# Memory keys of the first layer beside its attention, its modulation weights in a place of their own, and two heads in turn

## The reference, cut to what matters

```python
# first stack, layer l
mod = cond @ w_mod[l] + b_mod[l]                  # 6 x 1024: shift, scale and gate, twice
h = rms_norm(x, norm_mix[l]) * (1 + sc_a) + sh_a
mq, mk, mv, dq, dk, dv = split(h @ w_in[l])       # 8 plain heads of 64, 4 differential heads (2 x 64)
x = x + g_a * (concat(moba_attention(mq, mk, mv), diff_attention(dq, dk, dv)) @ w_out[l])
x = x + g_f * ((silu(h2 @ w_gate[l]) * (h2 @ w_up[l])) @ w_down[l])
# second stack, layer l
x = x + head_group_mixer(rmsnorm(x), w_in, ...)   # 8 stick-breaking heads of 64, 4 retention heads of 128
k, v = split(rmsnorm(mem, mem_norm[l]) @ wkv[l])  # "memory": 256 x 1024, an input of its own
x = x + cross_attention(rmsnorm(x), k, v)
x = x + peer_ffn(rmsnorm(x), ...)
# stick-breaking head: z = q k' / 8, causal
log_not_b = log_sigmoid(-z); a = exp(log_sigmoid(z) + reversed cumulative sum of log_not_b)
```

## Time and profile before

| | |
|---|---|
| median of 3 runs | 2847.84 us (2845.98 to 2852.53) |
| the profiled execution | 2845.72 us, span 2843.9 us |
| mean granted TensorE clock | 0.993 of full speed |
| TensorE busy | 2767.0 us, 97% of the span |
| VectorE busy | 2099.9 us, 74% |
| ScalarE busy | 1414.8 us, 50% |
| GpSimd busy | 195.7 us, 7% |
| read from HBM | 527.48 MB, 188 GB/s over the span |

### The profile page before, as it was taken

One profiled execution on the slowest core, in us unless ns is written; L12 is line 12 of the kernel. 1 busy time (PEld: TensorE's weight loads), 2 busy tenths in 40 slices (PEclk: granted clock), 3 DMA queues, 4 the chain that ended last, 5 costly groups with the idle time before them and its releaser, 6 DMA issues.

```text
span 2843.9 us, 40048 instructions
## 1 busy us (share of the span) xinstructions
PE 2767.0 (97%) x16458; PEld 2357.3 (83%) x16458; DVE 2099.9 (74%) x3106; ACT 1414.8 (50%) x1646; POOL 195.7 (7%) x172
## 2 busy tenths in 40 slices
PE   8989999999999999999999999999999999999998
PEld 7768888788888788888888888887888888888887
DVE  7877867665553679999879955536699999799655
ACT  4454445554456555554443344484555544443443
POOL 0200002010013001210000000030011200000000
PEclk9999999999999999999999999999999999999999
DMA  8857854555553355554445555633445544455554
GB/s 331 310 182 269 320 185 173 196 178 191 192 199 134 119 179 185 187 189 164 164 166 191 177 193 192 228 125 134 171 168 190 192 165 170 157 193 176 188 195 143
DMA packets 75637, 537.41 MB, mean 189 GB/s; under 512 B 8512, under 2 KB 8896, under 8 KB 12096
## 3 DMA queue, kind: packets, MB, share of 16 engines
q1 hardware_dynamic: 75456, 534.86, 53.9%
HBM read 527.48 MB, written 7.34 MB: 188 GB/s over the span
## 4 chain that ended last, share of the span: by engine, by line
PE 65%; issue 22%; DVE 7%; ACT 4%; DMA 2%; POOL 0%; SPq 0%; DVEq 0%; POOLq 0%; ACTq 0%
PE banks L442 18%; PE banks L450 9%; PE banks L516 7%; PE banks L519 7%; PE banks L527 7%; DVE wlo L1480 3%; PE banks L490 2%; ACT whi L999 2%; PE banks L492 2%; PE banks L501 2%; PE banks L464 2%; PE banks L466 2%; PE banks L474 1%; DMA raw<-in_wkv 1%; PE banks L944 1%
## 5 line engine op out<-in xcount | busy, mean ns | idle before, releaser
L999 ACT ACTIVATE whi<-raw 128x2048 fp32r<-128x2048 f32 x438 | 838.9, 1916 | 972.5 <-issue 813.8
L1480 DVE TENSOR_TENSOR wlo<-raw,whi 128x2048 fp32r<-128x2048 f32 x438 | 1006.8, 2299 | 312.5 <-ACT whi L999 297.3
L442 PE MATMUL banks<-ht,whi 128*128 128x512 f32 x2880 | 704.8, 394 | 8.5 <-DVE big L1554 2.8
L442 PEld LDWEIGHTS banks<-ht,whi 128*128 128x128 f32 x2880 | 527.6, 189 | 113.2 <-issue 6.6
L516 PE MATMUL banks<-whi,ht 128*128 128x512 f32 x1152 | 458.1, 398 | 13.5 <-DVE ht L1544 9.0
L519 PE MATMUL banks<-whi,ht 128*128 128x512 f32 x1152 | 452.7, 393 | 0.0
L450 PEld LDWEIGHTS banks<-ht,wlo 128*128 128x128 f32 x2880 | 369.1, 191 | 14.6
L450 PE MATMUL banks<-ht,wlo 128*128 128x256 f32 x2880 | 373.4, 282 | 0.0
L527 PE MATMUL banks<-wlo,ht 128*128 128x512 f32 x1152 | 290.6, 390 | 0.0
L516 PEld LDWEIGHTS banks<-whi,ht 128*128 128x128 f32 x1152 | 217.7, 189 | 58.9 <-issue 14.6
L519 PEld LDWEIGHTS banks<-whi,ht 128*128 128x128 f32 x1152 | 217.7, 189 | 43.2
(11 more groups left out here) (274 smaller groups left out, 3425.0 us busy)
## 6 DMA issues: line engine op xcount, KB each, us to landing
raw<-in_pu SPq DMA_DIRECT2D x128, 1024.0 KB, 4.9
raw<-in_pv SPq DMA_DIRECT2D x128, 1024.0 KB, 4.9
raw<-in_win SPq DMA_DIRECT2D x52, 1024.0 KB, 5.0
big<-in_wmod SPq DMA_DIRECT2D x24, 1024.0 KB, 6.6
raw<-in_wmod SPq DMA_DIRECT2D x24, 1024.0 KB, 5.0
raw<-in_wgate SPq DMA_DIRECT2D x22, 1024.0 KB, 4.9
raw<-in_wup SPq DMA_DIRECT2D x22, 1024.0 KB, 5.2
raw<-in_wdown SPq DMA_DIRECT2D x22, 1024.0 KB, 4.9
```

What stands on the lines that cost most here:

```text
L442: m = e.matmul(bank[b + n], h[:, q, c[n]], M.both[:, q * 512:(q + 1) * 512], start=q == 0, stop=False, skip_group_check=True)
L999: e.activation(whi(j), slot[u][0], ACT.Copy).then_inc(*hi.mark(j))
L1480: e.tensor_tensor(wlo(j), slot[u][0], whi(j).bitcast(F32), ALU.subtract).then_inc(*lo.mark(j))
```

## The change

It does three things. The four key units of layer 0 move from the opening into its attention, which now is laid out as that of layer 1 (eight units, two steps each); the memory's transposes move to nb 2 and their low part to nb 3, the lead units are fetched first, and one write of layer 0's keys and values replaces two. The 16 mid units leave the ring and share one slot, `LEAD[3]`, with the next fetched when VectorE has read the last; their places in the list are spread over units 0 to 19. And two heads are taken in turn, matmul by matmul: the plain heads of the first mixer, the logits and the retention scores of the second; there `sticks`, `stick_values`, `keep` and ScalarE's functions follow in pairs, with a ring of four in place of three. On VectorE, `columns(1, 0)` moves ahead of `down(i - 1)` at one place.

```diff
--- before.py
+++ after.py
-    m0, k0 = munits(0, 0), wunits("wkv", 0, 8)
-    units += [m0[0], m0[1], k0[0], m0[2], m0[3], k0[1], m0[4], m0[5], k0[2], m0[6], m0[7], k0[3]]
-    units += first_mixer(0, [0, 1, 3, 4, 6, 7, 9, 10, 11, 12, 12, 13, 13, 14, 14, 15], munits(0, 1) + munits(0, 2))
+    units += munits(0, 0)
+    units += first_mixer(0, [0, 1, 3, 4, 6, 7, 9, 10, 11, 12, 13, 14, 15, 16, 18, 19], munits(0, 1) + munits(0, 2))
...
-    main = [u for u in range(len(units)) if u not in {*lead, *side}]
+    mid = [u for u, x in enumerate(units) if x[0] == "m" and x[2:4] in ((0, 1), (0, 2))]
+    main = [u for u in range(len(units)) if u not in {*lead, *mid, *side}]
     slot = {u: (RAW[:, i % NRAW * UN:(i % NRAW + 1) * UN], i % NRAW, i // NRAW) for i, u in enumerate(main)}
     slot.update({u: (SIDE[i % 2], NRAW + i % 2, i // 2) for i, u in enumerate(side)})
     slot.update({u: (LEAD[i], NRAW + 2 + i, 0) for i, u in enumerate(lead)})
+    slot.update({u: (LEAD[3], NRAW + 10, i) for i, u in enumerate(mid)})
...
+    order_of.update({u: (mid, i, 1) for i, u in enumerate(mid)})
...
         def first_mixer(l):
             name = ("mix1", l)
             if l == 0:
-                warm(name, 7)
-                turn_all(("m", 0), MEM, DG[1])
-                for i in range(3):
-                    if i == 2:
-                        turn_all(name, XA, DG[0])
-                    a_unit(("K", 0, i), MT, lambda q: normed(on, ("m", 0), q), b=i - 1 if i == 2 else None)
-                for _ in column_sums(0, 0, 0):
+                turn_all(name, XA, DG[0])
+                on.wait_ge(*mac.at((0, 0, 5)))
+                warm(name, 7, 0)
+                for _ in column_sums(0, 0, 1):
                     pass
-                a_unit(("K", 0, 3), MT, lambda q: normed(on, ("m", 0), q), b=2)
             else:
                 gate_row(1, 0, (0, 1))
                 warm(name, 6)
...
-                if l and nb == 2:
+                if nb == 2:
                     for t in range(2):
                         on.wait_ge(*d_mem[t].at(l))
+                    on.wait_ge(*normal.at(("m", 0, "diag")))
                     for q in range(4):
                         turn(("m", l), q, MEM, DG[1], q)
...
             def step(i):
                 if i < 8:
-                    scores(0, (i,))
+                    if i % 2 == 0:
+                        scores(0, (i, i + 1))
                 elif i < 12:
                     scores(2, (2 * (i - 8), 2 * (i - 8) + 1))
...
                         if q % 4 == 3:
-                            step(f * n)
-                    b_unit([("V", l, f // 2, t) for t in range(2)], MT, f % 2, ready, b=(2, 3),
-                           between=None if l else lambda: step(f * n + 1))
+                            step(f * 2)
+                    b_unit([("V", l, f // 2, t) for t in range(2)], MT, f % 2, ready, b=(2, 3))
                 else:
-                    a_unit(("K", l, f - 4), MT, lambda q: normed(on, ("m", l), q), lambda: step(f * n),
+                    a_unit(("K", l, f - 4), MT, lambda q: normed(on, ("m", l), q), lambda: step(f * 2),
                            (2, 3, 0, 1)[f - 4])
-                if (f + 1) * n < 12 or l:
-                    step((f + 1) * n - 1)
-
-            n = 2 if l else 3
-            for f in range(8 if l else 4):
+                step(f * 2 + 1)
+
+            for f in range(8):
                 fill(f)
-            for i in range(16 if l else 11, 16):
-                step(i)
             project(("o1", l), ("mix1", l), OO)
 
         def out_part(name, o, q, b=None):
...
-            def logits(h):
-                b = clear(("sb", l, h), 2 + h % 2)
-                on.wait_ge(*took_v.at(("f", l, 2 * (h // 4) + 1)))
-                p0, c = 64 * (h % 2), h // 2
+            def logits(c):
+                for h in (2 * c, 2 * c + 1):
+                    clear(("sb", l, h), 2 + h % 2)
+                on.wait_ge(*took_v.at(("f", l, 2 * (c // 2) + 1)))
                 for i in range(3):
-                    q = AG[p0:p0 + 64, SBQ + c * 256 + (i > 0) * 128:][:, 0:128]
-                    k = AG[p0:p0 + 64, SBK + c * 256 + (i > 1) * 128:][:, 0:128]
-                    m = e.matmul(bank[b][:, i * 128:(i + 1) * 128], k, q, start=i == 0, stop=True, skip_group_check=True)
-                m.then_inc(*scored.mark(("sb", l, h)))
+                    for h in (2 * c, 2 * c + 1):
+                        p0 = 64 * (h % 2)
+                        q = AG[p0:p0 + 64, SBQ + c * 256 + (i > 0) * 128:][:, 0:128]
+                        k = AG[p0:p0 + 64, SBK + c * 256 + (i > 1) * 128:][:, 0:128]
+                        m = e.matmul(bank[2 + h % 2][:, i * 128:(i + 1) * 128], k, q, start=i == 0, stop=True,
+                                     skip_group_check=True)
+                        if i == 2:
+                            m.then_inc(*scored.mark(("sb", l, h)))
...
-                q = [AG[p0:p0 + 64, RQ + c * 512 + i * 256:][:, 0:256] for i in range(2)]
-                k = [AG[p0:p0 + 64, RK + c * 512 + i * 256:][:, 0:256] for i in range(2)]
+                q, k = ([[AG[64 * j:64 * j + 64, x + c * 512 + i * 256:][:, 0:256] for i in range(2)] for j in range(2)]
+                        for x in (RQ, RK))
                 for i in range(2):
-                    e.matmul(bank[b][:, 0:256], k[i][:, 0:128], q[i], start=i == 0, stop=i == 1, skip_group_check=True)
+                    for j in range(2):
+                        e.matmul(of[j][:, 0:256], k[j][i][:, 0:128], q[j][i], start=i == 0, stop=i == 1,
+                                 skip_group_check=True)
                 for i in range(2):
-                    m = e.matmul(bank[b][:, 256:384], k[i][:, 128:256], q[i][:, 128:256], start=i == 0, stop=i == 1,
-                                 skip_group_check=True)
-                m.then_inc(*scored.mark(("ret", l, h)))
+                    for j in range(2):
+                        m = e.matmul(of[j][:, 256:384], k[j][i][:, 128:256], q[j][i][:, 128:256], start=i == 0,
+                                     stop=i == 1, skip_group_check=True)
...
-                if 3 <= i < 11:
+                for h in {5: (0, 1), 7: (2, 3), 9: (4, 5), 10: (6, 7)}.get(i, ()):
+                    stick_values(h)
+                if i in (3, 5, 7, 9):
                     sticks(i - 3)
-                if 2 <= i < 10:
-                    logits(i - 2)
+                    sticks(i - 2)
+                if i in (2, 4, 6, 8):
+                    logits(i // 2 - 1)
                 if i == 11:
                     retention_scores(0)
-                    retention_scores(1)
                 if i == 12:
                     retention_values(0)
                     retention_values(1)
-                    retention_scores(2)
-                    retention_scores(3)
...
-                if i % n == 0 and i // n < (8 if l else 4):
+                if i % 2 == 0:
                     take()
-                if l == 0 and i == 13:
...
                         e.activation(ag(to + t * 512, 512), psum(key)[:, :], func, scale=RMS[:, t:t + 1]).then_inc(
                             *took_a.mark(key))
-                if 3 <= i < 11:
+                if i in (3, 5, 7, 9):
                     sticks(i - 3)
-                if 2 <= i < 10:
+                    sticks(i - 2)
+                if i in (2, 4, 6, 8):
                     logits(i - 2)
+                    logits(i - 1)
...
                 columns(l, 0)
-            turn_moved(name, l, 0, lambda: None, None if l else lambda: through(place_of[4] + 2))
+            turn_moved(name, l, 0, lambda: None, None if l else lambda: upto(0))
+
+            if l == 0:
+                lambda_sums()
 
...
-                        lambdas()
-                if l and nb == 3:
+                if l == 0 and nb == 2:
+                    lambdas()
+                if l == 0 and nb == 1:
+                    diag(("m", 0), 1, lambda: None)
+                if nb == 3:
                     for q in range(4):
                         rest(("m", l, q), COLS[:, l * 64 + 48:l * 64 + 56], MT)
                 if 1 <= nb <= 4:
...
                     rotary(i - 6)
-                if 3 <= i < 11:
-                    h = i - 3
+                for h in (i - 3, i - 2) if i in (3, 5, 7, 9) else ():
                     on.wait_ge(*took_a.at(("sb", l, h)))
-                    keep(ag(RING + (h % 3) * 768, 384), ("exp", l, h))
-                if 2 <= i < 10:
-                    h = i - 2
+                    keep(ag(RING + (h % 4) * 768, 384), ("exp", l, h))
+                for h in (i - 2, i - 1) if i in (2, 4, 6, 8) else ():
                     on.wait_ge(*took_v.at(("sb", l, h)))
-                    keep(ag(RING + (h % 3) * 768 + 384, 384), ("soft", l, h))
+                    keep(ag(RING + (h % 4) * 768 + 384, 384), ("soft", l, h))
+                if i in (6, 8):
+                    rotary(i - 6)
             head_inverse(("o2", l, 0), 8, 168)
```

(30 more changed lines are left out.)

144 lines of the change are left out of this document (52 added, 92 removed).

## The result

The changed kernel took 2882.2 us (median of 4 runs, 2874.3 to 2886.2) beside 2847.9 for the kernel before: ratio 1.0115, 95% interval 1.009 to 1.0139, so about 33 us slower. I had forecast 2842.4 with a range that ended at 2850. The profiled execution has a span of 2884.4 us and a mean granted clock of 0.985, where before had 2843.9 and 0.993.

A forecast was written before the change was run, and what follows sets the result against it. TensorE, busy for 97% of the span, was taken to bound the kernel. Opening with layer 0 -1.2, layer 1's pairs -3.0 and second mixers -1.2 gave -5.4 from 2847.8: 2842.4 us, range 2832 to 2850.

The forecast's parts named there:

- Second mixer, new waits: Second mixer: new TensorE waits of 6.0 us less one of 1.35 return 4.7 of 5.3 us saved, -0.6 a layer.
- For later pairs: Second mixer, sticks of later pairs: TensorE waits 0.5, 0.2 and 0.2 us for ScalarE's chain of the second head.
- 2.4 us: Second mixer: TensorE's wait at `stick_values(6)`, since GpSimd's cut-outs of pair 3 stand behind two rotaries of 4.2 us each.
- Gain eaten: Rival, chance 0.18: 1 us lost at each of three to five new waits, perhaps by the clock; -1 us, 2847.
- Work saved: Second mixer: paired logits save 3.4 us and paired retention scores 1.9 us of TensorE, together 5.3 us a layer.
- The opening: Opening and layer 0: projection begins at 38.8, 16.5 us earlier; output projection at 194.6 against 195.75, so -1.2 us.
- Layer 1's pairs: Layer 1's first mixer: four pairs of plain heads taken in turn save 2.7 to 3.3 us, say -3.0.
- costs VectorE nothing: Layer 0's feed-forward: `columns(1, 0)` ahead of a unit costs VectorE nothing, since the low part behind waits for that unit.
- no overlap: Rival, chance 0.02: pairs do not overlap in the second mixer, 5.3 us a layer not saved; 2853.
- the waits were not hidden: Rival, chance 0.27: new waits in layer 0's projection and the second mixer are mostly hidden; -12 us, 2836.
- The mid slot: Rival, chance 0.10: the mid units' one slot becomes the bound if landing takes over 6.2 us; +8, 2850.
- The drain: Rival, chance 0.01: each ScalarE table load brings a drain, 1.4 us idle, lengthening waits for the sticks; about 2875.

The follow-up runs named there:

- e5: The changed kernel with GpSimd's selects ahead of its rotary products and ScalarE's pair work ordered by step; 2840.3 us, ratio 0.9975 to the kernel before.
- e12: The kernel before with GpSimd products and VectorE operations added behind its last transfer, alone and at once; a product took 1.31 us alone, 3.25 beside low parts.
- e3: The changed kernel with GpSimd's selects of a pair's exponentials ahead of the rotary products; 2860.3 us, ratio 1.0052 to the kernel before.
- e4: The changed kernel with idle matmuls in the three long waits of each second mixer; 2863.4 us, ratio 1.0046 to the kernel before.
- e11: e5 with idle matmuls at two places of each first mixer; 2838.8 us, ratio 0.9959 to the kernel before.
- e2: The changed kernel with its second mixers put back as before; 2846.5 us, ratio 0.9987 to the kernel before.
- e6: The changed kernel with ScalarE's order by step alone, selects still behind the rotary products; 2853.6 us, ratio 1.0017 to the kernel before.
- e1: The kernel before with the second mixers' part of the change alone; 2881.7 us, ratio 1.0102.
- e7: The kernel before with the scores of two heads in turn in layer 1's first mixer alone; 2849.1 us, ratio 0.9998.
- e9: The kernel before with the fixed second mixers alone (pairs, ring of four, selects ahead, ScalarE by step); 2845.1 us, ratio 0.9972.

## Why the prediction was wrong

- **The step that failed** is "Second mixer, new waits": "So 6.0 - 1.35 = 4.7 us come back of 5.3: -0.6 a layer". The waits were 14.9 and not 6.0, and behind them stood some 6.5 us of lower clock, so 14.9 - 1.35 + 6.5 - 5.3 = 14.8 us a mixer were lost. Taken piece by piece:
- The 2.7 us ahead of `sticks(1)` were 2.59. That ScalarE's two chains follow one another, and with no drain behind a load, held (1.28 us, and the next begins at once).
- "For later pairs ... 0.5, 0.2 and 0.2": these three did not come. I had followed the cut-outs only. The same ScalarE queue holds the copy of the values for `stick_values(0)`, behind both chains and a high part: 4.46 us, which I had nowhere. e5 took 3.0 of them away by shortening the chain.
- "2.4 us" at `stick_values(6)` was 7.8. The place and the releaser were right; the price, "two rotaries of 4.2", was read from rows in which VectorE was idle. The hint stood in the earlier trace rows: the first product took 0.98 us, with a low part over it for 0.4, and its like 0.72. In the new order the rotaries run in a row, under whole low parts, and take turns with them (e12): 14.1 us for two in place of 8.4 makes 8.1 of the 2.4. (The sum "8.35 + 8.5 + 0.4" is 17.25 and not 17.4; nothing hangs on it.) e3 gave most of it back.
- **The clock.** "Gain eaten" priced a wait at 1 us lost behind it. It was 2.2 on average for the three long ones (e4: 6.5 a mixer).
- **Work saved:** the 5.3 us a layer held: twelve logits records took the time of six, and each two heads of retention scores 933.51 - 931.99 = 1.5 us in place of 2.47. It is why the fixed mixer is shorter than before's, by 3.9 us in e5's trace and by 5.5 in e11's. So the forecast that the pairs pay was right as a possibility; this order of the other engines threw it away.
- **The opening,** "38.8 + 153.1 + 5.7 - 3.0 = 194.6": 203.4 in the changed kernel's trace, 200.1 in e2's. The start was 1.9 late; the wait at `turn_query` was 2.5, not 3.9; a unit waits 2.2 for its low part; and behind these waits TensorE runs at the lower clock (0.66 from 70 to 75 us, 0.67 from 90 to 95). The 153.1 from layer 1 had one short stretch of it (0.83 from 570 to 580). Further on less is left: layer 1's projection begins at 437.4 in the mean of six traces with the new opening, pairs and columns (the changed kernel, e2 to e6) and at 440.3 in that of four without (before, e1, e7, e9). Less the columns' 3.7, that is some 1 us of loss by this estimate, in traces that spread over 5 and 12 us.
- **Layer 1's pairs:** -3.0 was -1.9 in the changed kernel's trace and -1.4 in e7's: ahead of later pairs TensorE waits for softmax results.
- **The columns:** "costs VectorE nothing" looked at VectorE alone. TensorE's next unit was waiting for them, 2.7 us in before's trace, and the edit is worth about 4 us. It hid the misses of the opening and the pairs: together the parts outside the second mixers came to -3.7 (interval -8.8 to +1.4), where I had -4.2. That the two figures are close is luck.
- The rivals: no overlap is refuted (0.94 us for twelve records), and the waits were not hidden. The mid slot did not bind (modulation weights landed in 5.0 us at the median up to 200 us, and only one low part behind a mid was waited for, 2.2 us). The drain had the sign right and its size near (2875), by a mechanism that the rows refute again.

Open: whether the opening is worth anything, and why the clock falls behind a given wait of 1.4 to 3.2 us in one execution and not in the next.

## What to carry to other kernels

Pairing work on TensorE doubles what the other engines get at once: order it by step across the pair, not head after head, and look in each of their queues for what stands behind the doubled piece. A duration read from a row holds only with the neighbours that it had: before moving GpSimd's two-operand work, see what VectorE does over it. A wait of several microseconds cost more than itself here, since the matmuls behind it ran at half the clock; keep such waits short, or put matmuls into them. And when a forecast of several parts comes out right, test the parts: an edit priced at nothing can carry what another part lost.

## What the runs showed of the hardware

- GpSimd's products and VectorE's low parts take turns instruction by instruction: 1.31 us alone, 3.25 side by side, with VectorE's 2.3 becoming 3.26 (e12). An operand of VectorE in PSUM avoids it (1.33); one operand in SBUF, scaled by a number, does not (2.19).
- Behind the waits of 4.5, 5.1 and 7.8 us in the second mixers the granted clock was at the lower level for some 4 to 8 us, in every trace with them; with matmuls in the waits it was not. Behind shorter waits it fell in some executions only: behind 2.6 us in the changed kernel and e3 in both layers, in e1 in layer 1 and not in layer 0 (1.00 to 860 us); behind 1.4 us in e7's layer 0, where the mixer took 115.6 us, and not in before's, 112.5 with the same program.
- Behind waits of 1.5 to 3.2 us in the first mixers it also fell in some executions only, which is a large part of the spread of 12 to 23 us among the runs of a kernel without fillers.
- On ScalarE, Abs needs no load of its own beside Exp or Ln, while going between Exp and Ln costs 1.28 us each way. Head by head this is three loads for a later pair, by step one; for the first pair four and two.
